# Load queue of the GLA output: modulation tiles ahead of the weight items of their steps

## The reference

```
mod = silu(c) @ mod_w[i] + mod_b[i]            # (1, 6*2048), six vectors per layer
sh_m, sc_m, g_m, sh_f, sc_f, g_f = split(mod, 6)
h = rmsnorm(x, norm_mix_g) * (1 + sc_m) + sh_m
y = gla_mixer(h, ...)                          # ends in  o @ gla_w_o
x = x + (1 + g_m) * y
h = rmsnorm(x, norm_ffn_g) * (1 + sc_f) + sh_f # then the FFN
```

## Time and profile before

| what | us |
|---|---|
| median of 3 runs | 2343.49 |
| lowest and highest | 2342.9, 2344.79 |
| the profiled execution | 2346.6 |
| its span, first to last instruction | 2344.6 |
| TensorE busy | 2286.0 (98%) |
| VectorE busy | 1842.2 (79%) |
| ACT busy | 1094.0 (47%) |
| memory moved | 632.91 MB, mean 270 GB/s |

### The profile page before, as it was taken

One profiled execution on the slowest core, in us unless ns is written; L12 is line 12 of the kernel. 1 busy time (PEld: TensorE's weight loads), 2 busy tenths in 40 slices (PEclk: granted clock), 3 DMA queues, 4 the chain that ended last, 5 costly groups with the idle time before them and its releaser, 6 DMA issues. The chain is left out here.

```text
span 2344.6 us, 26915 instructions
## 1 busy us (share of the span) xinstructions
PE 2286.0 (98%) x10824; PEld 1862.6 (79%) x10824; DVE 1842.2 (79%) x1801; ACT 1094.0 (47%) x1193; POOL 34.5 (1%) x98
## 2 busy tenths in 40 slices
PE   5999999999999999999999989999999999999998
PEld 1468887788887888888887789888888888888886
DVE  5868987898998988888988879988787556564566
ACT  2234433444554345543455655445664445544454
POOL 0020000000000000000000000000000000000000
PEclk8999999999999999999999999999999999999999
DMA  9957789797997998889978478886786555555554
GB/s 362 386 196 286 253 296 349 271 347 257 347 330 276 360 339 308 317 305 375 341 267 302 140 241 260 301 312 237 265 290 212 197 185 191 179 192 189 193 184 157
DMA packets 259808, 632.91 MB, mean 270 GB/s; under 512 B 23505, under 2 KB 32745, under 8 KB 233978
## 3 DMA queue, kind: packets, MB, share of 16 engines
q1 hardware_dynamic: 258050, 625.90, 75.2%
q10 hardware_dynamic: 1656, 5.60, 0.6%
HBM read 629.36 MB, written 2.10 MB: 269 GB/s over the span
## 5 line engine op out<-in xcount | busy, mean ns | idle before, releaser
L1228 DVE TENSOR_TENSOR w_lo<-raw,w_hi 128x2048 fp32r<-128x2048 f32 (+1 forms) x378 | 840.1, 2224 | 312.4 <-ACT w_hi L763 310.4
L763 ACT ACTIVATE w_hi<-raw 128x2048 fp32r<-128x2048 f32 (+1 forms) x378 | 703.5, 1863 | 675.9 <-DMA raw<-in_ffn_w_up_dram 238.2
L1995 PE MATMUL gm<-w_hi,h_hi 128*128 128x512 f32 x1816 | 720.6, 397 | 1.6 <-DVE h_lo L1356 1.6
L1996 PE MATMUL gm<-w_hi,h_lo 128*128 128x512 f32 x1816 | 708.0, 390 | 0.0
L2002 PE MATMUL gm<-w_lo,h_hi 128*128 128x512 f32 x1816 | 448.7, 389 | 0.0
L1245 DVE SCALAR_TENSOR_TENSOR acc<-mods,c_col,acc 128x2048 f32<-128x2048 f32 x180 | 422.0, 2344 | 2.8 <-DMA mods<-in_mod_w_dram 2.4
L1995 PEld LDWEIGHTS gm<-w_hi,h_hi 128*128 128x128 f32 x1816 | 341.2, 188 | 77.8 <-issue 4.4
L2002 PEld LDWEIGHTS gm<-w_lo,h_hi 128*128 128x128 f32 x1816 | 340.9, 188 | 70.8
L1996 PEld LDWEIGHTS gm<-w_hi,h_lo 128*128 128x128 f32 x1816 | 341.3, 188 | 69.8 <-issue 1.7
L1995 PE MATMUL gm<-w_hi,a_hi 128*128 128x512 f32 x674 | 266.6, 396 | 1.6 <-ACT w_hi L763 1.6
L1996 PE MATMUL gm<-w_hi,a_lo 128*128 128x512 f32 x674 | 262.6, 390 | 0.0
(11 more groups left out here) (293 smaller groups left out, 2066.6 us busy)
## 6 DMA issues: line engine op xcount, KB each, us to landing
raw<-in_ffn_w_up_dram SPq DMA_DIRECT2D x176, 1024.0 KB, 5.1
mods<-in_mod_w_dram SPq DMA_DIRECT2D x170, 1024.0 KB, 7.1
raw<-in_ffn_w_down_dram SPq DMA_DIRECT2D x64, 1024.0 KB, 5.1
raw<-in_gla_w_in_dram SPq DMA_DIRECT2D x48, 1024.0 KB, 5.2
mods<-in_kv_mod_w_dram SPq DMA_DIRECT2D x32, 1024.0 KB, 7.0
raw<-in_ffn_w_down_dram SPq DMA_DIRECT2D x32, 768.0 KB, 4.3
raw<-in_gla_w_o_dram SPq DMA_DIRECT2D x16, 1024.0 KB, 7.0
raw<-in_mla_w_o_dram SPq DMA_DIRECT2D x16, 1024.0 KB, 6.2
```

The costliest lines, as they stand in the source:

```text
L763: act.activation(w_hi[:, k % RAW, 0:words], raw[:, k % RAW, 0:words], ACT.Copy).then_inc(hi_made, 1)
L1228: dve.tensor_tensor(w_lo[:, k % RAW, 0:words], raw[:, k % RAW, 0:words], w_hi[:, k % RAW, 0:words].bitcast(F32), ALU.subtract).then_inc(lo ...
L1995: pe.matmul(o, hi_s[:, kt, tok], wh[:, j, :], start=kt == 0, stop=False)
L1996: pe.matmul(o, lo_s[:, kt, tok], wh[:, j, :], start=False, stop=False)
```

## The change

The rule `late` is dropped, so in the GLA output, as everywhere else, the modulation load of a step is issued before the item load of that step. The waits of both loads are what they were, and VectorE's, ACT's and TensorE's programs are untouched.

```diff
-                late = a["gla_out"].item <= n - AHEAD < a["up00"].item
-                if not late:
-                    for m in mod_at.get(n - AHEAD, ()):
-                        load_mod(*m)
+                for m in mod_at.get(n - AHEAD, ()):
+                    load_mod(*m)
...
                 load_item(n, src)
-                if late:
-                    for m in mod_at.get(n - AHEAD, ()):
-                        load_mod(*m)
```

## The result

The changed kernel takes 2367.3 us (median of 4 runs, 2366.7 to 2369.5) beside 2343.6 us for the kernel before (median of 4 runs, one more than in the table of the kernel before): 23.7 us more, a ratio of 1.0100 with a 95% interval of 1.0087 to 1.0112. The forecast was 2363.3 us in a range of 2352 to 2371.

What follows compares the result with a forecast made beforehand. TensorE, busy for 98% of the span, was taken as the bound, with VectorE and DMA nearly level in the section. Loop 18.8 + clock 1.0 = 19.8 us; 2343.5 + 19.8 = 2363.3 us, range 2352 to 2371.

Steps and rivals of the forecast that it cites:

- the loop: GLA output, steps 4 to 13: tile used, loads issued, w_hi, w_lo, tile used; 14.12 us for two steps.
- The odd loop: GLA output, odd steps 3 to 13: five turns and two chunk adds, 75.4 us, a loss of 18.8 us.
- Steps 2 and 3 at nothing: First two modulation loads of the GLA output: moving them ahead of the item loads costs 0 us.
- Through to the end: End of the GLA output: the delay passes whole through the closing add and norm boundary; TensorE stands about 6 us.
- Delays that don't compound: Rival for the GLA output: only the last late item counts, +5.2 us, about 2348.7 us; chance 0.04.
- Short landings: Rival for the GLA output: the second load of a pair lands earlier, +8 to +14 us, 2352 to 2357; chance 0.10.
- Not slower: Rival for the GLA output: earlier modulation tiles shorten VectorE's waits, gain at most 0.9 us, 2342.6 us; chance 0.04.
- The longer fall of the clock: Rival behind the GLA output: first FFN item pays the full 3.9 us at 1.2 GHz, 2366.2 us; chance 0.13.
- the term of 1.0 us for the clock: Norm boundary behind the GLA output: TensorE's lower clock after idling adds 1.0 us, between 0 and about 3.9.

Runs made afterwards that it cites:

- The turn of VectorE's order: The changed kernel, with VectorE taking each step's modulation tile ahead of w_lo: 2343.2 us, ratio 1.0003.
- the parities: Two runs: the kernel before, with the modulation load first only in odd steps of the GLA output (2364.8 us), or only in even steps (2352.5 us).
- the half tiles: The changed kernel, with modulation tiles of steps 2 to 13 of the GLA output loaded only in their first half: 2360.3 us.
- the odd steps alone: The kernel before, with the modulation load ahead of the item load only in steps 3, 5, 7, 9, 11 and 13 of the GLA output: 2364.8 us.
- a single late item at step 9: The kernel before, with the modulation load ahead of the item load in step 9 of the GLA output only: 2347.3 us, ratio 1.0021.
- step 4 alone: The kernel before, with the modulation load ahead of the item load in step 4 of the GLA output only: 2343.3 us, ratio 1.0006.
- even steps alone: The kernel before, with the modulation load ahead of the item load only in steps 2, 4, 6, 8, 10 and 12 of the GLA output: 2352.5 us.

## Why the prediction was right, and where not

**What bounds the section, and the loop.** Right, and nearly to the number. The odd loop was put at 75.4 us from step 3's tile to step 13's and took 75.2; the loss there at 18.8 and is 18.6. Each term stands in the rows of after: 0.4 us in the pairs, 7.1 to 7.2 in all nine landings, two pairs of 14.0 and 14.1 us and two with a chunk add of 16.5. The turn of VectorE's order shows that it is this loop, the parities that there are two of them, the half tiles that the landing is a term of it. The Trainium skill's price for a transfer (DMA: Bandwidth & Descriptors, anatomy of one DMA, for the gpsimd path) would have made the landing an estimated 6.4 and the whole loss 15.8, 14.8 of it in the loop; the rows decide for 7.2.

**Steps 2 and 3 at nothing.** Right: in the changed kernel step 3's tile starts 7.3 us behind step 2's, as before.

**Through to the end.** Right: the closing add follows the last tile at once (539.42), and nothing behind gives the time back. TensorE stood 4.5 us ahead of the reduction, 6 being forecast: its last item took 7.4 us in place of 5.4, since the first part of it ran at the low clock behind the wait of 3.45 us for `w_lo`. That, and 4.3 us in two waits for `w_hi`, were not priced; VectorE, which never waited for TensorE up to the closing add, hides them.

**The rivals.** Delays that don't compound: excluded by the odd steps alone, though a single late item at step 9 does behave that way. Short landings: excluded, 7.2 us although the traffic fell. Not slower: excluded at its own point, for step 4's pair went out at 457.08, once VectorE had ended step 2's tile (454.71 + 2.34 = 457.05). The longer fall of the clock, at 0.13, came too, on top of the loop and larger than it was priced. What was said against it, that VectorE and ACT pace the boundary, ended with VectorE's wait of 3.93 us for TensorE.

**The step that failed** is the term of 1.0 us for the clock, with its upper bound of 3.9. The boundary (C) lost 5.3 us in one trace and 4.2 in the other. The prediction priced only the first FFN item at 1.2 GHz and left out that the reduction itself, which stands ahead of it, runs at that level: 10.4 us in place of 5.5. It fitted beside VectorE's root and normalisation before and doesn't at half the clock; VectorE's wait of 3.93 us is this, and it makes 4.0 of the 5.3. The other 1.3 lie in the transposes and first items behind. With 18.6 for the loop the sum is 22.8 to 23.9, and 23.7 and 24.9 were measured. The Trainium skill's rule (TensorE: Matmul & The Clock Gate, Part 1), that idleness brings the lower clock, agrees with the 0.50 behind the wait of 4.53 us. The wait isn't needed for a fall, though: with step 4 alone the clock came to 0.50 with no gap ahead. How much of the 4.2 to 5.3 us an execution would have lost without the wait stays open.

## What to carry to other kernels

Before two loads change places in an in-order queue, write down what each waits for and in which order its consumer takes them. If the load that goes first waits for an engine whose own program needs the second load first, the two queues close a loop; its length over the number of steps that it goes forward is the pace, and it is compared with the bounding engine's. And when a new wait falls on TensorE, price what comes right behind it at half the clock, the light work first.

## What the runs showed of the hardware that was not expected

- The clock stayed at 0.50 for 15 us, 540 to 555, although TensorE had no gap there: it ran single-column reductions with matmuls of 352 columns between, then transposes, and from 552.69 on the first matmuls of 512 columns. It was back at 0.95 from 555 to 560.
- The clock also fell without a gap ahead: with step 4 alone it was 0.50 from 525 to 530 us, TensorE being busy throughout from 515 to 540. With even steps alone it stood at 1.00 over the same work, 530 to 550 us.
- Matmuls that fill a wait kept the clock at 1.00 while they ran (535 to 540 us), but the light reduction behind them still fell to 0.72 and then 0.50.
- A load of 1 MB issued 0.4 us behind another landed after 7.1 to 7.2 us in all nine cases after the change, at a DMA share of 0.81 and 0.71 over most of them, and after 7.2 in the one case of the rows before, at 515.2, with a share of 0.86 from 512 to 520; alone it took 5.0. Half as much ahead of it made 6.1.
